# Feed-forward output product by seven block products in place of eight, in two of its three parts

## The chip, the cores and the metric

The kernel runs on one core of a Trainium2 chip. The metric is the device time of one launch in microseconds. Before the change the median of three runs is 2927.22 us (2925.56 to 2929.83).

## What is computed

A decoder trunk of two layers is applied to 512 prompt rows and to 8 sequences of 8 sample rows, 576 token columns in all, with a model width of 1024. Everything is float32. The change touches only the two feed-forward blocks of each layer:

```
D_MODEL = 1024
FFN_HIDDEN = 2816
def swiglu(x, w_in, w_out):
    gate, up = jnp.split(x @ w_in, 2, axis=-1)
    return (jax.nn.silu(gate) * up) @ w_out
...
x = x + 0.5 * swiglu(rms_norm(x, p['ffn1_norm']), p['ffn1_w_in'], p['ffn1_w_out'])
...                                   # mixers
x = x + 0.5 * swiglu(rms_norm(x, p['ffn2_norm']), p['ffn2_w_in'], p['ffn2_w_out'])
```

## The kernel before

Activations lie transposed: 128 channels on the partitions, 576 token columns (`N`) in the free dimension, two halves of 288 (`HF`). A float32 product is made of three products of rounded parts. Each weight tile and each activation is split into a high part (`whi`, `hh`, `ah`, a rounded copy by ScalarE) and a low part (`wlo`, `hl`, `al`, the original minus the high part, by VectorE); TensorE adds high x high, high x low and low x high (`project`, line 464). A tile is 128 output channels: for each of its chunks of 128 input channels three products in two halves, six matmuls of 288 columns. The two halves go to the two banks of one of four PSUM buffers `ps`.

Weights come in units of 1 MB (1024 x 256 values), two tiles each, into the two slots of `wraw` (`load`, line 356, on SyncE's queue). A unit is asked for when both tiles of the unit in the same slot have been split. Two slots of `whi` and `wlo` hold two split tiles; while TensorE works on one tile the tile two further on is split as soon as its slot is free (`split_ahead`, line 795 on ScalarE and line 1053 on VectorE).

The hidden width 2816 is worked off in three parts of 8, 8 and 6 chunks (`make_plan`). A part has a gates stage and an output stage. In the gates stage each step makes four tiles, two of the gate and two of the up projection; VectorE scales them by the row norm (line 1087), ScalarE takes Silu (line 827), VectorE multiplies (line 1095) and splits the result into `ah` and `al` (lines 1097, 1099). The output stage multiplies the part's chunks with `w_out` into eight output tiles, 8 chunks x 6 = 48 matmuls each, and VectorE adds half of each to `x` (line 1069). GpSimd only adds squares for the norms (line 1473) and issues stores. All order is written out by hand: each engine runs its own program in the order of the code, and semaphores (`filled`, `freed`, `lo_ready`, ...) tie them. After the first part of the first block SyncE also issues 16 small loads (`past_forgets`, line 382).

There are 2 layers x 2 blocks x 2 parts of 8 chunks: eight output stages with 1024 intermediate rows.

## Time and profile before

| | us |
|---|---|
| median of three runs | 2927.22 |
| the profiled execution's own time | 2922.63 |
| its span | 2921.0 |
| TensorE busy | 2876.8 (98%) |
| VectorE busy | 1462.1 (50%) |
| ScalarE busy | 986.9 (34%) |
| GpSimd busy | 118.5 (4%) |

The span is the time between the first and the last recorded instruction of the profiled execution; its own time is 1.6 us longer. Busy time counts an instruction's recorded duration; matmuls overlap each other in the pipeline, so the distance between two of them is shorter than the recorded duration of one.

### The profile page before, as it was taken

What the parts mean: (1) busy time and instruction counts of PE and PEld (TensorE: products, weight loads), DVE (VectorE), ACT (ScalarE), POOL (GpSimd) and SP (SyncE); (2) the same over time, 40 slices, a digit from 0 to 9 for tenths busy, and PEclk for the clock granted to TensorE, in tenths of its full rate; (3) what the DMA queues carried; (4) which work ended last, traced back from release to release, by engine and by line L of the source; (5) the groups of instructions that cost most, each with busy time, mean ns of one, the idle gap of its engine ahead of it and who ended that gap; (6) DMA issues with size and microseconds to landing.
All of it is one profiled execution on the core that took longest, in us unless ns stands there. A gap on an engine that the chain in (4) does not pass through costs nothing.

```text
span 2921.0 us, 55041 instructions
## 1 busy us (share of the span) xinstructions
PE 2876.8 (98%) x21664; PEld 2815.2 (96%) x21664; DVE 1462.1 (50%) x2025; ACT 986.9 (34%) x1295; POOL 118.5 (4%) x104
## 2 busy tenths in 40 slices
PE   7999999999999999999999999999999999999999
PEld 6999999898899999999999999998889999999998
DVE  4434356677545444343554343576665444444444
ACT  4212123555533332111332211335554333321124
POOL 1000001000000010000100000100000001000001
PEclk9999999999999999999999999999999999999999
DMA  3222223333222222222222222233332222222222
GB/s 119 86 75 84 87 72 99 89 93 89 79 79 86 86 87 76 83 86 74 86 83 78 87 87 86 73 89 89 95 102 67 86 79 94 77 83 87 84 75 90
DMA packets 299022, 248.82 MB, mean 85 GB/s; under 512 B 20643, under 2 KB 296307, under 8 KB 298919
## 3 DMA queue, kind: packets, MB, share of 16 engines
q1 hardware_dynamic: 296775, 242.44, 26.9%
q0 software_dynamic: 2144, 4.98, 0.5%
q8 instruction: 68, 1.11, 0.2%
q14 instruction: 35, 0.29, 0.0%
HBM read 240.04 MB, written 7.34 MB: 85 GB/s over the span
## 4 chain that ended last, share of the span: by engine, by line
PE 95%; DVE 2%; issue 1%; ACT 1%; DVEq 1%; DMA 0%; POOLq 0%; ACTq 0%; SPq 0%
PE ps L464 87%; PE ps L630 1%; PE ps L568 1%; PE ps L569 1%; PE ps L570 1%; PE ps L648 1%; PE ps L610 1%; DVE tmp L1059 1%; PE ps L695 0%; PE ps L617 0%; PE ps L632 0%; DMA xin<-in_x_sample 0%; PE ps L663 0%; ACT whi L795 0%; POOLq L1471 0%
## 5 line engine op out<-in xcount | busy, mean ns | idle before, releaser
L795 ACT ACTIVATE whi<-wraw 128x1024 fp32r<-128x1024 f32 x452 | 471.9, 1045 | 1554.6 <-PE ps L464 1542.7
L464 PE MATMUL ps<-hh,whi 128*128 128x288 f32 x4480 | 965.9, 297 | 11.7 <-DVE wlo L1053 5.3
L464 PE MATMUL ps<-hl,whi 128*128 128x288 f32 x4480 | 959.1, 296 | 0.0
L464 PE MATMUL ps<-hh,wlo 128*128 128x288 f32 x4480 | 959.1, 296 | 0.0
L1053 DVE TENSOR_TENSOR wlo<-wraw,whi 128x1024 fp32r<-128x1024 f32 x452 | 543.9, 1204 | 401.1 <-ACT whi L795 400.3
L464 PEld LDWEIGHTS ps<-hh,whi 128*128 128x128 f32 x4480 | 722.5, 189 | 14.5 <-DVE wlo L1053 6.3
L464 PEld LDWEIGHTS ps<-hl,whi 128*128 128x128 f32 x4480 | 722.7, 189 | 0.0
L464 PEld LDWEIGHTS ps<-hh,wlo 128*128 128x128 f32 x4480 | 722.3, 189 | 0.0
L1087 DVE TENSOR_TENSOR tmp<-tmp,ps 128x576 f32<-128x576 f32 x176 | 132.6, 753 | 505.3 <-PE ps L464 504.3
L464 PE MATMUL ps<-ah,wlo 128*128 128x288 f32 x1408 | 302.2, 296 | 0.0
L464 PE MATMUL ps<-ah,whi 128*128 128x288 f32 x1408 | 302.2, 296 | 0.0
L464 PE MATMUL ps<-al,whi 128*128 128x288 f32 x1408 | 302.1, 296 | 0.0
L1069 DVE SCALAR_TENSOR_TENSOR x<-ps,x 128x576 f32 x112 | 84.8, 757 | 351.7 <-PE ps L464 351.7
L464 PEld LDWEIGHTS ps<-ah,whi 128*128 128x128 f32 x1408 | 227.4, 189 | 0.0
L464 PEld LDWEIGHTS ps<-al,whi 128*128 128x128 f32 x1408 | 227.4, 188 | 0.0
L464 PEld LDWEIGHTS ps<-ah,wlo 128*128 128x128 f32 x1408 | 227.4, 188 | 0.0
L795 ACT ACT_TABLE_LOAD x32 | 41.1, 1283 | 143.6 <-PE ps L464 143.5
L1469 POOL COPY tmp<-tmp 128x576 f32<-128x576 f32 x7 | 6.7, 952 | 2039.9 <-ACT tmp L815 2024.6
L1473 POOL TENSOR_TENSOR tmp<-tmp 128x576 f32<-128x576 f32 x49 | 82.5, 1685 | 156.9 <-ACT tmp L815 155.3
L464 PE MATMUL ps<-ol,whi 128*128 128x288 f32 x384 | 82.5, 296 | 0.0
L464 PE MATMUL ps<-oh,whi 128*128 128x288 f32 x384 | 82.4, 296 | 0.0
L464 PE MATMUL ps<-oh,wlo 128*128 128x288 f32 x384 | 82.3, 296 | 0.0
(296 smaller groups left out, 2425.1 us busy)
## 6 DMA issues: line engine op xcount, KB each, us to landing
wraw<-in_ffn_w_in SPq DMA_DIRECT2D x88, 1024.0 KB
wraw<-in_ffn_w_out SPq DMA_DIRECT2D x32, 1024.0 KB
wraw<-in_w_in SPq DMA_DIRECT2D x28, 1024.0 KB
wraw<-in_w_in SPq DMA_DIRECT2D x56, 512.0 KB
wraw<-in_ffn_w_out SPq DMA_DIRECT2D x16, 768.0 KB
wraw<-in_w_branch SPq DMA_DIRECT2D x24, 512.0 KB
wraw<-in_w_out SPq DMA_DIRECT2D x9, 1024.0 KB
kv<-in_cache_k SPq DMA_DIRECT2D x128, 64.0 KB, 1.9
```

Of the source, the lines that this page charges most:

```text
L464: last = pe.matmul(ps[slot][:, half, 0:HF], weights, rhs[:, k, half * HF:(half + 1) * HF], start=(start and c == 0 and n == 0), stop=(stop ...
L568: pe.matmul(out, hh[:, k, tok], rh, start=(k == 0), stop=False)
L569: pe.matmul(out, hl[:, k, tok], rh, start=False, stop=False)
L570: last = pe.matmul(out, hh[:, k, tok], rl, start=False, stop=(k == KD - 1))
L610: last = pe.matmul(ps[pr.slot(k)][:, half, 0:HF], bones, tmp[k - 3][:, half * HF:half * HF + HF], start=True, stop=True)
L630: pe.matmul(logits(e, qb), qp[hs, qs], kp[hs, 0:n], start=True, stop=False, skip_group_check=True)
L648: last = pe.matmul(ps[pr.slot(k)][:, half, 0:XB // 2], wab[:, k - 13, :], tmp[3][:, half * (XB // 2):(half + 1) * (XB // 2)], start=True, ...
L795: act.activation(split_tile(into, j, rowwise), raw_tile(slot, j, rowwise), ACT.Copy).then_inc(hi_ready, 1)
L1053: dve.tensor_tensor(split_tile(lo, j, rowwise), raw_tile(slot, j, rowwise), split_tile(hi, j, rowwise).bitcast(F32), ALU.subtract).then_in ...
L1069: dve.scalar_tensor_tensor(out=two(xm), in0=cols(st.slot(k)), scalar=half, in1=two(xm), op0=ALU.mult, op1=ALU.add)\
L1087: dve.tensor_tensor(two(pf[:, 0:N]), two(tmp[6][:, 0:N]), cols(st_in.slot(k)), ALU.mult)\
L1473: pool.tensor_tensor(tmp[6][:, 0:N], tmp[6][:, 0:N], tmp[2 + m % 2][:, 0:N], ALU.add).then_inc(sq_added, 1)
```

## The change

In the first two parts of each block the output product (1024 outputs x 1024 intermediate rows x 576 columns) is done by Strassen's scheme. One unit of `w_out` (256 outputs x 1024 intermediate rows) is taken as 2 x 2 blocks of 128 outputs x 512 rows, the intermediate values as 2 x 2 blocks of 512 rows x 288 columns. Seven products of sums of blocks replace eight products of blocks. One product is 4 chunks x 3 parts = 12 matmuls of 288 columns, a unit is 84 matmuls in place of 96, a stage of four units 336 in place of 384.

- GpSimd makes the four sums of weight blocks (`weight_sums`) in `wsum`, one instruction of 512 elements each. A sum may overwrite its buffer when the low part of the former unit's has been made.
- ScalarE and VectorE split seven weight blocks of 512 elements per unit (`comb_split`) in place of two tiles of 1024, into a ring of four, four products ahead.
- The activations are kept as seven splits (`bh`, `bl`: B11, T1, T2, T3, B21, B22, T4, where T1 to T4 are differences) in place of `ah`, `al`. VectorE makes the differences and the low parts, ScalarE the high parts, in the gates stage (`gates_seven`). Chunks 0 to 3 hold the upper row blocks, so B11 and T1 are complete after them; the other five need chunks 4 to 7.
- The products run into three banks, `a`, `c` and `b`, in the order a, c, a, c, a, b, a. The partial sum in bank `a` or `c` is copied out by ScalarE (0.5 times it) before the next product adds to the same bank; VectorE adds banks and copies to `x` (`out_seven`). In total VectorE has, per unit, three additions of 288 elements from PSUM and three of copies (288, 576, 288), where it had two of 576.
- The next load of `w_out` is released when the last block of the unit two before has been split. The next stage's tiles are split after products 25 and 27.
- `lfp` moves to another place in SBUF, and VectorE waits for the state stores before the second block and not behind it.

```diff
+M_B11, M_T1, M_T2, M_T3, M_B21, M_B22, M_T4 = range(7)
+MOVING = (M_B11, M_T1, M_T2, M_B22, M_T3, M_B21, M_T4)
+DONE_NO = {0: 1, 1: 2, 2: 3, 4: 4, 5: 5}
+COPY_NO = {2: 1, 3: 2, 4: 3, 6: 4}
...
+            bh = sb("bh", [P, 7, 4, HF], F32R, m)
+            bl = sb("bl", [P, 7, 4, HF], F32R, m)
+            kept = sb("kept", [P, 4, 3, HF], F32, m)
+            wsum = sb("wsum", [P, 4, 4 * P], F32, m)
...
+        def ring(buf, q):
+
+            r = q % 4
+            return buf[:, r // 2, r % 2 * 4 * P:(r % 2 + 1) * 4 * P].rearrange("p (k c) -> p k c", c=P)
...
+            def seven(st, g, L):
+
+                for u in range(4):
+                    i, k0 = u // 2, 2 * (u % 2)
+                    first, second = ps[st.slot(k0)], ps[st.slot(k0 + 1)]
+                    a, b, c = first[:, 0, 0:HF], first[:, 1, 0:HF], second[:, 0, 0:HF]
+                    for m, bank in enumerate((a, c, a, c, a, b, a)):
+                        q = 7 * u + m
+                        if m < 6:
+                            pe.wait_ge(comb_lo, L * 96 + (24 * g + 6 * u + m + 1))
+                        else:
+                            pe.wait_ge(lo_ready, st.unit(0, L) * 2 + (2 * u + 2 + AHEAD))
+                        if m < 2:
+                            wait_psum(st, k0 + m, L, i)
+                        if m in COPY_NO:
+                            pe.wait_ge(part_copied, L * 64 + (16 * g + 4 * u + COPY_NO[m]))
+                        if q == 0:
+                            pe.wait_ge(mov_ready, L * 64 + (16 * g + 4))
+                        wh, wl = ring(whi, q), ring(wlo, q)
+                        x_ = MOVING[m]
+                        for kk in range(4):
+                            if u == 0 and m >= 2:
+                                pe.wait_ge(mov_ready, L * 64 + (16 * g + 4 + 3 * kk + (1 if x_ in (M_T2, M_T3) else 3 if x_ == M_T4 else 2)))
+                            for t, (weights, moving) in enumerate(((wh, bh), (wh, bl), (wl, bh))):
+                                last = pe.matmul(bank, weights[:, kk, :], moving[:, x_, kk, :], start=(m in (0, 1, 5) and kk == 0 and t == 0),
+                                                 stop=(m in (3, 5, 6) and kk == 3 and t == 2), skip_group_check=True)
+                        if m == 3:
+                            last.then_inc(filled[st.slot(k0 + 1)], 1)
+                        elif m == 6:
+                            last.then_inc(filled[st.slot(k0)], 1)
+                        else:
+                            last.then_inc(product_done, 1)
...
+            def comb_split(st, g, q, L):
+
+                u, m = divmod(q, 7)
+                if m in (0, 5, 6):
+                    raw_loaded(st, u, L)
+                else:
+                    act.wait_ge(wsum_ready, L * 64 + (16 * g + 4 * u + m))
+                ins = act.activation(ring(whi, q), weights_of(st, u, m), ACT.Copy)
+                if m < 6:
+                    ins.then_inc(comb_hi, 1)
+                else:
+                    ins.then_inc(hi_ready, 2)
...
+                for u in range(4):
+                    i, k0 = u // 2, 2 * (u % 2)
+                    first, second = ps[st.slot(k0)], ps[st.slot(k0 + 1)]
+                    one, other = scratch(u)
+                    for m in range(7):
+                        q = 7 * u + m
+                        if m == 3:
+                            wait_tile(st, k0 + 1, L, i)
+                        elif m == 6:
+                            wait_tile(st, k0, L, i)
+                        else:
+                            act.wait_ge(product_done, L * 80 + (20 * g + 5 * u + DONE_NO[m]))
+                        if m == 0:
+                            act.activation(one[:, 0:HF], first[:, 0, 0:HF], ACT.Copy, scale=0.5).then_inc(part_copied, 1)
+                        elif m == 1:
+                            act.activation(other[:, HF:N], second[:, 0, 0:HF], ACT.Copy, scale=0.5).then_inc(part_copied, 1)
+                        elif m == 2:
+                            act.activation(one[:, HF:N], first[:, 0, 0:HF], ACT.Copy, scale=0.5).then_inc(part_copied, 1)
+                        elif m == 4:
+                            act.activation(other[:, 0:HF], first[:, 0, 0:HF], ACT.Copy, scale=0.5).then_inc(part_copied, 1)
+                        if q == 1:
+                            moving_late(g, 3, L)
+                        if q + 4 < 28:
+                            comb_split(st, g, q + 4, L)
+                        elif q == 25:
+                            split_ahead(st, 2, None, L, 1)
+                        elif q == 27:
+                            split_ahead(st, 3, None, L, 1)
+                        if q == 0:
+                            moving_sums(g, 3, L)
...
+            def moving_lo(g, at, a, b, c, raw, L):
+
+                dve.wait_ge(mov_hi, L * 64 + (16 * g + at + 1))
+                dve.tensor_tensor(bl[:, a:b, c, :], raw, bh[:, a:b, c, :].bitcast(F32), ALU.subtract).then_inc(mov_ready, 1)
...
+            def gates_seven(st, st_out, g, s0, L):
+
+                for i in range(4):
+                    for k in range(4):
+                        wait_tile(st, k, L, i)
+                        pf = tmp[k if k < 2 else 2 + k]
+                        dve.tensor_tensor(two(pf[:, 0:N]), two(tmp[6][:, 0:N]), cols(st.slot(k)), ALU.mult).then_inc(freed[st.slot(k)], 1)
+                        if k < 2:
+                            split_ahead(st, k, L, i)
+                            continue
+                        c = 2 * i + k - 2
+                        dve.drain()
+                        dve.wait_ge(silu_ready, L * 44 + (s0 + i * 2 + k - 1))
+                        if c < 4:
+                            dve.tensor_tensor(kept[:, c, 0:2, :], two(pf[:, 0:N]), two(tmp[k - 2][:, 0:N]), ALU.mult)
+                            dve.drain()
+                            dve.tensor_tensor(kept[:, c, 2, :], kept[:, c, 1, :], kept[:, c, 0, :], ALU.subtract).then_inc(mov_raw, 1)
+                            split_ahead(st, k, L, i)
+                            moving_lo(g, c, M_B11, M_T1 + 1, c, kept[:, c, 0:3:2, :], L)
+                            continue
+                        kk = c - 4
+                        dve.tensor_tensor(pf[:, 0:N], pf[:, 0:N], tmp[k - 2][:, 0:N], ALU.mult)
+                        dve.drain()
+                        dve.tensor_tensor(tmp[2][:, 0:HF], pf[:, HF:N], kept[:, kk, 2, :], ALU.subtract)
+                        dve.tensor_tensor(tmp[2][:, HF:N], pf[:, HF:N], kept[:, kk, 1, :], ALU.subtract).then_inc(mov_raw, 1)
+                        dve.drain()
+                        dve.tensor_tensor(tmp[3][:, 0:HF], pf[:, 0:HF], tmp[2][:, 0:HF], ALU.subtract).then_inc(mov_raw, 1)
+                        if i < 3:
+                            split_ahead(st, k, L, i)
+                        else:
+                            comb_split(st_out, g, 2 * k - 4, L)
+                        moving_lo(g, 4 + 3 * kk, M_T2, M_T3 + 1, kk, two(tmp[2][:, 0:N]), L)
+                        if i == 3:
+                            comb_split(st_out, g, 2 * k - 3, L)
+                        moving_lo(g, 5 + 3 * kk, M_B21, M_B22 + 1, kk, two(pf[:, 0:N]), L)
+                        moving_lo(g, 6 + 3 * kk, M_T4, M_T4 + 1, kk, tmp[3][:, 0:HF].rearrange("p (a n) -> p a n", a=1), L)
...
+                        if m == 3:
+                            wait_tile(st, k0 + 1, L, i)
+                            dve.scalar_tensor_tensor(out=up[:, HF:N], in0=second[:, 0, 0:HF], scalar=0.5, in1=up[:, HF:N], op0=ALU.mult, op1=ALU.add)\
+                                .then_inc(freed[st.slot(k0 + 1)], 1)
+                        elif m == 5:
+                            dve.wait_ge(product_done, L * 80 + (20 * g + 5 * u + 5))
+                            dve.scalar_tensor_tensor(out=up[:, 0:HF], in0=first[:, 1, 0:HF], scalar=0.5, in1=up[:, 0:HF], op0=ALU.mult, op1=ALU.add)
+                            dve.wait_ge(part_copied, L * 64 + (16 * g + 4 * u + 4))
+                            dve.tensor_tensor(down[:, HF:N], down[:, HF:N], other[:, 0:HF], ALU.add)
+                            dve.drain()
+                            dve.tensor_tensor(up, up, one[:, 0:N], ALU.add)
+                            dve.tensor_tensor(down[:, HF:N], down[:, HF:N], other[:, HF:N], ALU.add)
+                        elif m == 6:
+                            dve.drain()
+                            wait_tile(st, k0, L, i)
+                            dve.scalar_tensor_tensor(out=down[:, 0:HF], in0=first[:, 0, 0:HF], scalar=0.5, in1=down[:, 0:HF], op0=ALU.mult, op1=ALU.add)\
+                                .then_inc(freed[st.slot(k0)], 1)
+                        if q + 4 < 28:
+                            comb_split(st, g, q + 4, L)
+                        elif q == 25:
+                            split_ahead(st, 2, L, 1)
+                        elif q == 27:
+                            split_ahead(st, 3, L, 1)
...
+                dve.wait_ge(f_stored, L * 96 + 96)
                 ffn("ffn2", 2, L)
-
-                dve.wait_ge(f_stored, L * 96 + 96)
 
...
+            def weight_sums(st, g, L):
+
+                for u in range(4):
+                    base = st.first_unit + u
+                    slot = base % 2
+                    a11, a12, a21, a22 = (block_of(slot, kh, mh_) for mh_ in range(2) for kh in range(2))
+                    wait_apart(pool, unit_loaded[slot], L * (plan["layer_units"] // 2 * 32) + (base // 2 + 1) * 32)
+                    for j, (x0, x1, op) in enumerate(((a21, a22, ALU.add), (summed(0), a11, ALU.subtract), (a12, summed(1), ALU.subtract),
+                                                      (a11, a21, ALU.subtract))):
+                        if u:
+                            wait_apart(pool, comb_lo, L * 96 + (24 * g + 6 * u - 4 + j))
+                        pool.tensor_tensor(summed(j), x0, x1, op).then_inc(wsum_ready, 1)
+                        pool.drain()
+
             add_squares(0)
             with pool.Fori(0, DEPTH) as L:
+                for part in range(2):
+                    weight_sums(S["ffn1"][part][1], part_no(0, part), L)
```

The order of the instructions at three places. First TensorE at the start of an output stage of 1024 rows, before (`ah` and `al` are the intermediate values, ps1 a PSUM buffer of two banks):

```order
L450 ISA [waits lo_ready]
L504 ISA [waits freed1]
L464 MATMUL ps1<-ah,whi 128x288 [waits a_ready]
L464 MATMUL ps1<-ah,whi 128x288
L464 MATMUL ps1<-al,whi 128x288 x2
L464 MATMUL ps1<-ah,wlo 128x288 x2
```

and now, where product 0 goes to ps1, product 1 to ps2 and product 2 to ps1 again:

```order
L494 REGISTER_ALU [waits comb_lo]
L543 REGISTER_ALU [waits freed1]
L550 MATMUL ps1<-bh,whi 128x288 [waits mov_ready]
...
L550 MATMUL ps2<-bh,whi 128x288 [waits freed2,comb_lo]
...
L541 REGISTER_ALU [waits comb_lo]
L548 REGISTER_ALU [waits part_copied]
L550 MATMUL ps1<-bh,whi 128x288 [waits mov_ready]
```

A product has 12 matmuls where a tile had 48, and each product waits for its own weight block (`comb_lo`) and from product 2 on for the copy of its bank (`part_copied`).

Second, VectorE from the last tile of a gates stage on, before (tmp5 is the up projection, tmp1 the Silu of the gate):

```order
L1087 TENSOR_TENSOR tmp5<-tmp6,ps0 128x576 [waits filled0]
L1094 REGISTER_ALU
L1095 TENSOR_TENSOR tmp5<-tmp5,tmp1 128x576 [waits silu_ready]
L1097 ISA
L1097 COPY ah<-tmp5 128x576
L1099 REGISTER_ALU
L1099 TENSOR_TENSOR al<-tmp5,ah 128x576
L1052 REGISTER_ALU
L1053 TENSOR_TENSOR wlo<-wraw,whi 128x1024 [waits hi_ready]
```

and now (the `wlo` rows are the low parts of the weight blocks of products 2, 3 and 4):

```order
L1268 TENSOR_TENSOR tmp5<-tmp6,ps0 128x576 [waits filled0]
...
L1283 TENSOR_TENSOR tmp5<-tmp5,tmp1 128x576 [waits silu_ready]
L1285 TENSOR_TENSOR tmp2<-tmp5,kept 128x288
L1286 TENSOR_TENSOR tmp2<-tmp5,kept 128x288
L1288 TENSOR_TENSOR tmp3<-tmp5,tmp2 128x288
...
L1251 TENSOR_TENSOR wlo<-wsum,whi 128x512 [waits comb_hi]
...
L1260 TENSOR_TENSOR bl<-tmp2,bh 128x2x288 [waits mov_hi]
...
L1251 TENSOR_TENSOR wlo<-wsum,whi 128x512 [waits comb_hi]
...
L1260 TENSOR_TENSOR bl<-tmp5,bh 128x2x288 [waits mov_hi]
...
L1260 TENSOR_TENSOR bl<-tmp3,bh 128x288 [waits mov_hi]
...
L1251 TENSOR_TENSOR wlo<-wsum,whi 128x512 [waits comb_hi]
```

Three differences and the low parts of three groups of activations stand between the tile and the weight blocks of products 2 to 4.

Third, GpSimd, which before had nothing in these stages; now the four sums of a stage's first unit and two of its second (`wsum` is written, `wraw` are the loaded weights):

```order
L1740 TENSOR_TENSOR wsum<-wraw 128x512 [waits unit_loaded0,pre_done]
L1740 TENSOR_TENSOR wsum<-wsum,wraw 128x512
L1740 TENSOR_TENSOR wsum<-wraw,wsum 128x512
L1740 TENSOR_TENSOR wsum<-wraw 128x512
L286 ISA [waits unit_loaded1,pre_done]
L1740 TENSOR_TENSOR wsum<-wraw 128x512 [waits comb_lo,pre_done]
L286 REGISTER_ALU
L1740 TENSOR_TENSOR wsum<-wsum,wraw 128x512 [waits comb_lo,pre_done]
```

The first unit's sums wait for its load alone; those of each later unit also for the low parts of the unit before.

## Rows read from the trace of the kernel before

**Rows 1.** The page: span, busy time by engine, granted clock in 40 slices.

```profile
span 2921.0 us, 55041 instructions
...
PE 2876.8 (98%) x21664; PEld 2815.2 (96%) x21664; DVE 1462.1 (50%) x2025; ACT 986.9 (34%) x1295; POOL 118.5 (4%) x104
...
PEclk9999999999999999999999999999999999999999
```

**Rows 2.** The page: chain that ended last, by engine and by line.

```profile
PE 95%; DVE 2%; issue 1%; ACT 1%; DVEq 1%; DMA 0%; POOLq 0%; ACTq 0%; SPq 0%
PE ps L464 87%; PE ps L630 1%; PE ps L568 1%; PE ps L569 1%; PE ps L570 1%; PE ps L648 1%; PE ps L610 1%; DVE tmp L1059 1%; PE ps L695 0%; PE ps L617 0%; PE ps L632 0%; DMA xin<-in_x_sample 0%; PE ps L663 0%; ACT whi L795 0%; POOLq L1471 0%
```

**Rows 3.** Timeline, TensorE, first output product and next gates (start us, us, what).

```profile
135.48 0.42 PE L464 MATMUL ps<-ah,whi 128*128 128x288 f32 x2
...
186.68 0.43 PE L464 MATMUL ps<-hh,whi 128*128 128x288 f32 x2
```

**Rows 4.** Timeline, VectorE, last gate tile and first output tile of that stage.

```profile
135.68 0.75 DVE L1087 TENSOR_TENSOR tmp<-tmp,ps 128x576 f32<-128x576 f32 x1 [1.80 <-PE ps L464]
136.60 0.76 DVE L1095 TENSOR_TENSOR tmp<-tmp 128x576 f32<-128x576 f32 x1 [0.16 <-issue]
...
138.15 0.76 DVE L1099 TENSOR_TENSOR al<-tmp,ah 128x576 f32 x1
138.83 1.22 DVE L1053 TENSOR_TENSOR wlo<-wraw,whi 128x1024 fp32r<-128x1024 f32 x1
142.20 0.76 DVE L1069 SCALAR_TENSOR_TENSOR x<-ps,x 128x576 f32 x1 [2.16 <-PE ps L464]
```

**Rows 5.** Timeline, ScalarE, a whole split and a Silu in the gates.

```profile
123.20 1.06 ACT L795 ACTIVATE whi<-wraw 128x1024 fp32r<-128x1024 f32 x1 [1.75 <-PE ps L464]
124.17 0.67 ACT L827 ACTIVATE tmp<-tmp 128x576 f32<-128x576 f32 x1
```

**Rows 6.** Timelines, VectorE and ScalarE near 540; last row by line: smaller shapes.

```profile
540.56 0.45 DVE L1356 TENSOR_TENSOR tmp<-tmp,ps 128x288 f32<-128x288 f32 x1
...
542.10 0.68 DVE L1053 TENSOR_TENSOR wlo<-wraw,whi 128x512 fp32r<-128x512 f32 x1
...
540.25 0.63 ACT L795 ACTIVATE whi<-wraw 128x512 fp32r<-128x512 f32 x1 [1.18 <-PE ps L464]
...
L892 ACT ACTIVATE vtok<-ps,small 128x256 f32<-128x256 f32 x20 | 7.9, 477 | 17.9 <-PE ps L570 17.7
```

**Rows 7.** Timelines, GpSimd and VectorE, end of the first row of squares.

```profile
26.50 1.40 POOL L1473 TENSOR_TENSOR tmp<-tmp 128x576 f32<-128x576 f32 x1 [0.16 <-issue]
...
27.65 1.34 DVE L1148 TENSOR_TENSOR wlo<-wraw,whi 128x1024 fp32r<-128x1024 f32 x1 [11.77 <-ACT whi L857]
```

**Rows 8.** Timelines, VectorE and GpSimd near 458; last row by tile: vlo (min/median/max ns).

```profile
457.94 0.82 DVE L1074 SCALAR_TENSOR_TENSOR hl<-x,gains,hh  x1
459.23 3.04 DVE L1053 TENSOR_TENSOR vlo<-wraw,vhi 128x1024 fp32r<-128x1024 f32 x2 [0.47 <-ACT vhi L795]
...
458.32 1.72 POOL L1473 TENSOR_TENSOR tmp<-tmp 128x576 f32<-128x576 f32 x1 [3.06 <-ACT tmp L815]
...
L1053 DVE TENSOR_TENSOR vlo<-wraw,vhi x4: 1212/1558/1904, 459.2 to 1901.0; 128x1024 fp32r<-128x1024 f32 x4
```

**Rows 9.** Timelines, SyncE queue; then windows of 1 us, last two columns DMA share, GB/s.

```profile
152.85 18.34 SPq L382 DMA_DIRECT2D lfp<-in_cache_logf  x16
...
189.45 0.40 SPq L356 DMA_DIRECT2D wraw<-in_ffn_w_in  x1
...
193.00:194.00 1.00, 1.00 (x10) 1.00 (x9) 0.74 (x1) 0.59 (x1) 0.00 (x0) 1.00 0.89 299
194.00:195.00 1.00, 1.00 (x10) 1.00 (x9) 0.51 (x2) 1.00 (x2) 0.00 (x0) 1.00 0.06 16
```

**Rows 10.** Timeline, TensorE, product of the values, 256 columns into one bank.

```profile
463.07 0.28 PE L570 MATMUL ps<-wlo,hh 128*128 128x256 f32 x1
463.19 0.28 PE L568 MATMUL ps<-whi,hh 128*128 128x256 f32 x1
463.31 0.28 PE L569 MATMUL ps<-whi,hl 128*128 128x256 f32 x1
```

More of the change, by code:

```diff
@@ L212, in build @@
                 cs = sb("cs", [P, PAST + ST], F32, m2)
-                lfp = sb("lfp", [P, NPG, 2 * NS], F32, m2)
                 lf = sb("lf", [F_W, N], F32, m2)
@@ L221, in build @@
                 prow = sb("prow", [P, NR], F32, m2)
+                lfp = sb("lfp", [P, NPG, 2 * NS], F32, m2)
             with ExitStack() as m2:
@@ L309, in split_tile, with block_of, summed, weights_of @@
             return buf[:, j, 0:n * P].rearrange("p (k c) -> p k c", c=P)
+        def ring(buf, q):
+            r = q % 4
+            return buf[:, r // 2, r % 2 * 4 * P:(r % 2 + 1) * 4 * P].rearrange("p (k c) -> p k c", c=P)
+        def block_of(u, kh, mh_):
+            return wraw[:, u, :].rearrange("p (k c) -> p k c", c=256)[:, 4 * kh:4 * kh + 4, mh_ * P:mh_ * P + P]
+        def summed(j):
+            return wsum[:, j, :].rearrange("p (k c) -> p k c", c=P)
+        def weights_of(st, u, m):
+            slot = (st.first_unit + u) % 2
+            if m == 0:
+                return block_of(slot, 0, 0)
+            if m == 5:
+                return block_of(slot, 1, 0)
+            if m == 6:
+                return block_of(slot, 1, 1)
+            return summed(m - 1)
+        def scratch(u):
+            return tmp[(0, 4)[u % 2]], tmp[(1, 5)[u % 2]]
+        def part_no(n, part):
+            return 2 * (n // 2) + part
         def ahead(st, k):
@@ L820, in ffn @@
                 for part, (st_in, st_out, kc) in enumerate(S[name]):
+                    if part < 2:
+                        gates_seven(st_in, st_out, part_no(n, part), L)
+                        out_seven(st_out, part_no(n, part), L)
+                        done += kc
+                        continue
                     with act.Fori(0, st_in.steps) as i:
@@ L1076, in update, with comb_split @@
                                 .then_inc(h_ready, 1)
+            def comb_split(st, g, q, L):
+                u, m = divmod(q, 7)
+                if m < 6:
+                    dve.wait_ge(comb_hi, L * 96 + (24 * g + 6 * u + m + 1))
+                else:
+                    dve.wait_ge(hi_ready, st.unit(0, L) * 2 + (2 * u + 2))
+                ins = dve.tensor_tensor(ring(wlo, q), weights_of(st, u, m), ring(whi, q).bitcast(F32), ALU.subtract)
+                if m < 6:
+                    ins.then_inc(comb_lo, 1)
+                else:
+                    ins.then_inc(lo_ready, 2)
@@ new lines, in out_seven @@
+            def out_seven(st, g, L):
+                for u in range(4):
+                    i, k0 = u // 2, 2 * (u % 2)
+                    first, second = ps[st.slot(k0)], ps[st.slot(k0 + 1)]
+                    one, other = scratch(u)
+                    up, down = x[:, 2 * u, :], x[:, 2 * u + 1, :]
+                    for m in range(7):
+                        q = 7 * u + m
+                        if m == 3:
[21 more added lines that the diff above has]
+                            split_ahead(st, 3, L, 1)
@@ L1081, in ffn @@
                 for part, (st_in, st_out, kc) in enumerate(S[name]):
+                    if part < 2:
+                        gates_seven(st_in, st_out, part_no(n, part), 22 * (n // 2) + done, L)
+                        out_seven(st_out, part_no(n, part), L)
+                        done += kc
+                        continue
                     with dve.Fori(0, st_in.steps) as i:
@@ L1515, in _ @@
                 add_squares(L * 24 + 16)
+                for part in range(2):
+                    weight_sums(S["ffn2"][part][1], part_no(2, part), L)
                 add_squares(L * 24 + 24)
```

61 lines of the change are left out of this document (49 added, 12 removed).

## The prediction

> **What bounds the kernel now.** I read the page first: TensorE is busy for 98% of the span at the full granted clock, VectorE for 50%, GpSimd for 4% [rows 1]. The chain that ended last is TensorE for 95%, nearly all at the one line of the split products [rows 2]. So a matmul fewer is time gained as long as TensorE's stream stays closed, and the other engines have spare time on average. The timeline of TensorE gives the price: the first output stage runs from 135.48 to 186.68, 51.20 us for 8 tiles x 48 = 384 matmuls, 133.3 ns each [rows 3], and VectorE, ScalarE and the loads wait for it. Then I read the timelines of VectorE and ScalarE at the stage's start for what stands between the last gate tile and the first products [rows 4, 5], the smaller shapes [rows 6], and the places where GpSimd and VectorE work at once [rows 7, 8], since the change makes them do so in every stage.
>
> **What goes.** Each of the eight stages loses 384 - 336 = 48 matmuls: 48 x 133.3 ns = 6.40 us, 51.2 us in all. The shape (288 columns, 128 x 128 weights, a weight load for each) is the same. One product is 12 matmuls, 1.60 us; a unit 11.2 us; a stage 44.8 us.
>
> The Trainium skill (TensorE: Matmul & The Clock Gate, Back-to-back issue gap) gives N/2.4 + 2.5 ns for a lone warm gap, 122.5 ns at 288 columns; by it the saving would be 47.0 us. The row has 133.3 ns, and I go by the row.
>
> **What each engine must do in a unit.** An instruction that follows another on VectorE starts about 0.08 us before the former's recorded end (138.15 + 0.76 against 138.83) [rows 4], so its cost in a row is 0.60 for 512 elements (0.68), 0.37 for 288 (0.45) and 0.68 for 576 (0.76) [rows 4, 6]. A wait for the pipe between dependent ones adds about 0.17 (136.60 after 135.68 + 0.75). VectorE: seven weight blocks 4.2, three additions from PSUM 1.1, three additions of copies 1.4, two such waits 0.3: 7.0 of 11.2 us. ScalarE: seven blocks of 0.55, four copies that I put at 0.4 (128x256 from PSUM took 0.48, 128x512 from SBUF 0.63 [rows 6]): 5.5 us. A copy has one product's time, 1.6 us, before its bank is needed: hidden. The longest row on VectorE, behind product 5, is 2.7 us and stands against the 4.8 us of three products by which the ring is ahead: hidden. GpSimd: a sum of 576 elements took 1.40 us beside an idle VectorE [rows 7]. I take 0.12 of it as start (below), 1.28 as work, and by elements 1.14 for 512. Not seen is whether a block read from `wraw` (128 of each 256 values) costs more; bounds are 1.14 (in proportion) and 1.60 (the 1.72 recorded for 576 in rows 8, less the start). I take 1.14, since the 1.72 is explained by a wait.
>
> **Loads.** A load was asked for at 189.45 and its last full window of traffic is 193 to 194 [rows 9]: about 4.6 us. The load of unit u+2 is now released at the end of product 7u+2 plus about 1.5 us and lands 6.1 us behind that product; ScalarE wants it after product 7u+10, 12.8 us behind. Covered. SyncE's 16 small loads hold its queue for 18.34 us once per layer [rows 9]; they now start near 153.5 and end near 172, the next stage's first unit lands near 177, and it is wanted at 135.5 + 26 x 1.6 = 177.1. Between nothing and 1 us, twice; I take 0. The stage's end: ScalarE can split the next gates' first tile from product 25's end on, VectorE is done 0.4 + 1.06 + 1.22 and some 0.15 for two hand-overs later [rows 4 to 6], 2.8 us against 3.2 until TensorE wants it: covered by 0.4. The earlier wait for the state stores and the place of `lfp` cost nothing: both are long over when asked for.
>
> **The stage's start, if engines didn't hinder each other.** Zero is the first product's start (135.48). VectorE takes up the last gate tile at 0.20 and begins the second multiplication at 1.12 [rows 4]. Then 0.76 and a wait of 0.19; two differences 0.37 + 0.45 + 0.17; the third 0.37; the low part of product 2's weights starts at 3.44 and ends at 4.12. TensorE wants it at 3.20 and goes on at 4.2: 1.0 us idle. Behind it in VectorE's row stand low parts of 576, 512, 576, 288, 512 elements; product 3's block is ready at 5.4 (wanted at 5.8), product 4's at 7.05 (wanted at 7.4). Net gain 6.4 - 1.0 = 5.4 us a stage.
>
> **What GpSimd's sums do to it.** The rows show each engine standing still while the other holds something. VectorE's 1024-element low part, median 1.22 us elsewhere, took 1.34 when begun at 27.65, and ended 1.09 behind GpSimd's end at 27.90 [rows 7]; of two begun at 459.23 (3.04 us in place of 2.36) the first waited for GpSimd, which ended at 460.04, and the tile's maximum is 1.90 against a minimum of 1.21 [rows 8]. The other way round, GpSimd's sum begun at 458.32 ended 1.28 us behind VectorE's end at 458.76 [rows 8]; alone it takes 1.40, hence the 0.12 above. All these have two inputs in SBUF; VectorE's PSUM readers are not among them.
>
> Per unit VectorE then needs the shared way for 4.2 + 1.4 = 5.6 us and GpSimd for 4 x 1.14 = 4.6: 10.2 of 11.2 us. That fits, and three products of lead soak up the turns once a stage runs. At its start there is no lead. The second unit's sums are released one by one by low parts 1, 2 and 3 of the first, so each comes at the worst time. Sum 0 takes the way from -0.45 to 0.69, the last low part of the gate chunk before goes behind it, and VectorE reaches the gate tile at 1.06 in place of 0.20: product 2's block is ready at 5.0, 1.8 us late. Sum 1 comes before product 3's block (ready at 7.4, wanted at 6.6 by now): 0.8. Sum 2 comes before the low part of T4 (product 4's block ready at 10.2, wanted at 9.0): 1.2. In all 3.8 us idle, a net gain of 6.4 - 3.8 = 2.6 us a stage.
>
> Rows 7 and 8 show one waiting instruction at a time; here VectorE has the next one ready when it ends, and the sum above lets the engine that has waited longer go first. The Trainium skill (SBUF — State Buffer, Who interferes with whom) says that whichever issues first has the shared pair for the whole instruction and the other blocks fully; by that the turns are as I took them, and the change comes to -21 us rather than the -43 of a VectorE that is never held up.
>
> **The sum.** 8 x (6.40 - 3.8) = 20.8 us. The profiled execution's 2922.6 becomes 2901.8; the median of the runs before lies 4.6 above that execution, so I say 2906.
>
> **Rivals.**
> First, VectorE isn't held up: its instructions follow so closely that GpSimd only gets in where VectorE waits anyway. For it: VectorE's instructions in a row overlap by 0.08 us. Against it: rows 7 and 8. It gives 8 x 5.4 = 43 us, 2884; if the 1.0 us goes too, 2876.
> Second, slower than before: GpSimd's sums are long and the shared way becomes the bound. At 1.60 us a sum the unit needs 5.6 + 6.4 = 12.0 us of it; the three units with sums of their own in the stage lose 0.8 each, and the start's three blockades grow by 0.46 each: 3.8 + 2.4 + 1.4 = 7.6 us against the 6.4 gained, +1.2 x 8 = 10 us, 2937. It decides from about 1.45 us a sum, where nothing is left. For it: the strided reads. Against it: 1.28 for 576 elements twice over.
> Third, gain and loss nearly cancel: sums of 1.3 to 1.4, or restarts of TensorE, late loads after the small ones and the narrow 0.4 us at each stage's end together take 1.5 to 2.6 us more a stage. It gives 2919 to 2927.
> Fourth, the products cost more than 133.3 ns a matmul, since 12 follow each other into one bank where before two banks took turns. Against it: in the values' product the matmuls of 256 columns all go to one bank and start 0.11 to 0.12 us apart [rows 10], 118.5 in proportion. I leave it a small chance inside the third case.
>
> **How the numbers follow.** Forecast 0.50 (2898 to 2915 on its own), first rival 0.20, third with fourth 0.18, second 0.12. A measurement tells 0.2%, 5.9 us, from no change. Faster: 0.50 + 0.20 + 0.06 = 0.76; same: 0.11 of the third case and 0.02 of the second, 0.13; slower: 0.11. The range from 2880 to 2932 takes in the first rival at 2884 and the third case, and leaves out the second rival's far end.
>
> **What would show it.** Output stages of 48 to 49 us (44.8 of products, the rest idle before products 2, 3 and 4 of the first unit, put down to VectorE's line 1251) show the sum right. VectorE's instructions there above 1.2 us with GpSimd beside them, and GpSimd's sums of 1.26 alone and up to 1.9 queued, show the shared way. Stages near 46 us speak for the first rival; idle time before products in units 2 and 3 with `wsum` behind it for the second; waits of ScalarE on a load for an error in the loads; a distance of matmuls over 134 ns within a product for the fourth. The prediction is wrong if the stall is not at the stage's start.

## The result, and the profile after

| | before | after |
|---|---|---|
| median of four runs, us | 2927.74 (2925.56 to 2929.83) | 2907.86 (2903.64 to 2909.55) |
| ratio, with its 95% interval | | 0.9933 (0.9919 to 0.9948) |
| profiled execution's span | 2921.0 | 2907.9 |

The forecast was 2906 us. The page of the kernel after answers to [rows 1, 2]:

```profile
span 2907.9 us, 56195 instructions
...
PE 2837.9 (98%) x21280; PEld 2770.5 (95%) x21280; DVE 1708.7 (59%) x2441; ACT 1131.7 (39%) x1683; POOL 312.1 (11%) x232
...
PE 88%; DVE 5%; issue 3%; SPq 1%; DVEq 1%; ACT 1%; DMA 1%; POOLq 0%; ACTq 0%
```

TensorE's share of the chain that ended last has gone from 95% to 88%, VectorE's from 2% to 5%. Of the 51.2 us of removed matmuls 18.5 are left in the eight stages of this execution (below); the rest, almost two thirds, has come back as waiting. Where it waits is seen in the timeline of TensorE through an undisturbed output stage (start us, us, what, and in brackets the idle time before with what ended it), which answers to [rows 3]:

```profile
290.65 0.29 PE L550 MATMUL ps<-bh,whi 128*128 128x288 f32 x1
...
295.49 0.39 PE L550 MATMUL ps<-bh,whi 128*128 128x288 f32 x1 [1.46 <-DVE wlo L1251]
...
297.83 0.39 PE L550 MATMUL ps<-bh,whi 128*128 128x288 f32 x1 [0.49 <-ACT tmp L966]
...
300.59 0.38 PE L550 MATMUL ps<-bh,whi 128*128 128x288 f32 x1 [0.91 <-DVE wlo L1251]
...
339.06 0.43 PE L508 MATMUL ps<-hh,whi 128*128 128x288 f32 x2
```

The stage takes 48.41 us, from 290.65 to 339.06, in place of 51.20. Counted from 0 as in the prediction, product 2 was due at 293.87 and began 1.62 late, product 3 (due 297.09) 0.74 late, product 4 (due 299.43) 1.16 late: 3.5 us idle. From there 24 products run without a gap in 38.47 us. Product 4 takes 1.67 of it, since a first matmul behind a stop takes some 0.08 longer; the other 23 take 1.600 each, 133.3 ns a matmul as before. VectorE and GpSimd over the same time, which answer to [rows 4, 8]:

```profile
288.78 0.68 DVE L1251 TENSOR_TENSOR wlo<-wsum,whi 128x512 fp32r<-128x512 f32 x1
289.38 2.21 DVE L1260 TENSOR_TENSOR bl<-tmp,bh 128x576 fp32r<-128x576 f32 x2
291.51 0.74 DVE L1268 TENSOR_TENSOR tmp<-tmp,ps 128x576 f32<-128x576 f32 x1
...
294.55 0.68 DVE L1251 TENSOR_TENSOR wlo<-wsum,whi 128x512 fp32r<-128x512 f32 x1
295.15 0.75 DVE L1260 TENSOR_TENSOR bl<-tmp,bh 128x576 fp32r<-128x576 f32 x1
295.82 1.79 DVE L1251 TENSOR_TENSOR wlo<-wsum,whi 128x512 fp32r<-128x512 f32 x1
297.53 2.22 DVE L1260 TENSOR_TENSOR bl<-tmp,bh 128x576 fp32r<-128x576 f32 x2
299.67 0.68 DVE L1251 TENSOR_TENSOR wlo<-wsum,whi 128x512 fp32r<-128x512 f32 x1
```

```profile
289.60 1.67 POOL L1740 TENSOR_TENSOR wsum<-wraw 128x512 f32<-128x512 f32 x1 [9.23 <-DVE wlo L1251]
295.38 1.67 POOL L1740 TENSOR_TENSOR wsum<-wsum,wraw 128x512 f32<-128x512 f32 x1 [4.11 <-DVE wlo L1251]
297.75 1.67 POOL L1740 TENSOR_TENSOR wsum<-wraw,wsum 128x512 f32<-128x512 f32 x1 [0.70 <-DVE wlo L1251]
```

The low part at 288.78 releases GpSimd's sum, which starts at 289.60 while VectorE is inside its next instruction. It waits for that one and then holds VectorE's following one until 291.27, so VectorE reads the last gate tile at 291.51. The same is seen at 295.82: a low part of 512 elements takes 1.79 in place of 0.68. It ends 0.56 behind the sum's end at 297.05. The third stop comes from the pair at 297.53, which takes 2.22 beside the sum at 297.75 (1.12 where no sum is read, below) and pushes back the low part at 299.67.

The bracket of product 3 names ScalarE's copy, but TensorE's program (`seven`) asks there only for the copy before that one. The three low parts end at 295.23, 297.61 and 300.35 and the products start 0.26, 0.22 and 0.24 later: all three waited for VectorE.

The eight output stages take, in order, 50.12, 48.41, 48.53, 48.40, 50.27, 48.39, 48.53, 48.43 us: 391.1 in place of 409.6. The first and the fifth, the ones of each layer with the 16 small loads, are 1.8 longer. SyncE's queue (two rows), ScalarE (one) and TensorE (one) at the end of the first, against [rows 9]:

```profile
161.69 18.38 SPq L426 DMA_DIRECT2D lfp<-in_cache_logf  x16
180.60 1.99 SPq L400 DMA_DIRECT2D wraw<-in_ffn_w_in  x2
```

```profile
185.70 2.04 ACT L875 ACTIVATE whi<-wraw 128x1024 fp32r<-128x1024 f32 x2 [1.85 <-DMA wraw<-in_ffn_w_in]
```

```profile
188.16 0.53 PE L508 MATMUL ps<-hh,whi 128*128 128x288 f32 x2 [1.56 <-DVE wlo L1219]
```

The small loads hold the queue until 180.07, the next gates' unit lands near 185.7, and TensorE stands still for 1.6 to 1.7 us.

**Where the profiled pair's 13.1 us come from.** The stages give 18.5. Two things work against it, by the distance of the gate tiles on VectorE (left out here: the rows between) in the first gates stage, before and after:

```profile
60.80 0.76 DVE L1087 TENSOR_TENSOR tmp<-tmp,ps 128x576 f32<-128x576 f32 x1 [1.81 <-PE ps L464]
...
67.04 0.75 DVE L1087 TENSOR_TENSOR tmp<-tmp,ps 128x576 f32<-128x576 f32 x1 [1.88 <-PE ps L464]
```

```profile
61.44 0.76 DVE L1268 TENSOR_TENSOR tmp<-tmp,ps 128x576 f32<-128x576 f32 x1 [2.37 <-PE ps L508]
...
67.84 0.76 DVE L1268 TENSOR_TENSOR tmp<-tmp,ps 128x576 f32<-128x576 f32 x1 [2.38 <-PE ps L508]
```

6.24 us a tile before, 6.40 after, at a granted clock of 1.00 in both: 2.56 us in each layer's first gates stage. At the start of layer 2 TensorE idled 1.9 us and then ran at 0.50 (1.2 GHz) for about 3.3 us, which cost 1.5 (24 matmuls of 288 columns took 4.81 us, and 3.29 behind the stop of 2.7 us at the same place in layer 1, where the clock stayed at 1.00):

```profile
1479.00:1480.00 1.00, 0.04 (x1) 1.00 0.00 0
1480.00:1481.00 1.00, 1.00 (x7) 0.85 0.00 0
1481.00:1482.00 1.00, 1.00 (x6) 0.50 0.00 0
...
1483.00:1484.00 1.00, 1.00 (x6) 0.50 0.63 181
1484.00:1485.00 1.00, 1.00 (x9) 0.94 1.08 383
```

(Columns: stretch, its length, TensorE busy, granted clock, DMA share, GB/s.) In layer 1 the stretch from the second output stage's end to the third's start, mostly mixers, is 1.4 shorter; in the second profile of the kernel before it is 1.1 shorter too, so most of that belongs to the execution. 18.5 - 5.1 - 1.5 + 1.4 = 13.3, near the 13.1. The medians differ by 19.9, near the 18.5 of the stages, and the second profiles of both kernels, at the end of the experiments, show why.

### The profile page after: what moved, and what is told of

It reads as the page before. It is cut to its first block, busy times and chain, and to the rows that moved or that the text cites. A ratio compares the mean times of both kernels' runs of the same rounds, so it can differ in the third digit from the quotient of the medians.

```text
span 2907.9 us, 56195 instructions
## 1 busy us (share of the span) xinstructions
PE 2837.9 (98%) x21280; PEld 2770.5 (95%) x21280; DVE 1708.7 (59%) x2441; ACT 1131.7 (39%) x1683; POOL 312.1 (11%) x232
## 3 DMA queue, kind: packets, MB, share of 16 engines
q8 instruction: 79, 1.29, 0.2%
## 4 chain that ended last, share of the span: by engine, by line
PE 88%; DVE 5%; issue 3%; SPq 1%; DVEq 1%; ACT 1%; DMA 1%; POOLq 0%; ACTq 0%
PE ps L508 72%; PE ps L550 8%; DVE bl L1260 1%; PE ps L710 1%; DVE wlo L1251 1%; PE ps L650 1%; PE ps L649 1%; PE ps L648 1%; PE ps L728 1%; PE ps L690 1%; SPq L426 1%; DVE tmp L1225 1%; SPq L424 1%; PE ps L775 0%; PE ps L697 0%
## 5 line engine op out<-in xcount | busy, mean ns | idle before, releaser
L875 ACT ACTIVATE whi<-wraw 128x1024 fp32r<-128x1024 f32 (+1 forms) x388 | 403.8, 1041 | 1144.4 <-PE ps L508 1118.0
L1219 DVE TENSOR_TENSOR wlo<-wraw,whi 128x1024 fp32r<-128x1024 f32 (+1 forms) x388 | 466.8, 1203 | 388.5 <-ACT whi L875 387.7
L550 PE MATMUL ps<-bh,whi 128*128 128x288 f32 x896 | 267.0, 298 | 23.0 <-DVE wlo L1251 18.9
L550 PE MATMUL ps<-bh,wlo 128*128 128x288 f32 x896 | 266.7, 298 | 0.0
L550 PE MATMUL ps<-bl,whi 128*128 128x288 f32 x896 | 265.2, 296 | 0.0
L550 PEld LDWEIGHTS ps<-bh,whi 128*128 128x128 f32 x896 | 168.4, 188 | 28.3 <-issue 28.3
L550 PEld LDWEIGHTS ps<-bl,whi 128*128 128x128 f32 x896 | 169.1, 189 | 0.0
L550 PEld LDWEIGHTS ps<-bh,wlo 128*128 128x128 f32 x896 | 168.3, 188 | 0.0
L1251 DVE TENSOR_TENSOR wlo<-wraw,whi 128x512 fp32r<-128x512 f32 x96 | 112.6, 1189 | 17.1 <-ACT whi L908 16.8
L1251 DVE TENSOR_TENSOR wlo<-wsum,whi 128x512 fp32r<-128x512 f32 x128 | 114.0, 893 | 6.7 <-ACT whi L908 6.1
```

Of the source, the lines that this page charges most:

```text
L550: last = pe.matmul(bank, weights[:, kk, :], moving[:, x_, kk, :], start=(m in (0, 1, 5) and kk == 0 and t == 0), stop=(m in (3, 5, 6) and ...
L875: act.activation(split_tile(into, j, rowwise), raw_tile(slot, j, rowwise), ACT.Copy).then_inc(hi_ready, 1)
L1219: dve.tensor_tensor(split_tile(lo, j, rowwise), raw_tile(slot, j, rowwise), split_tile(hi, j, rowwise).bitcast(F32), ALU.subtract).then_in ...
L1251: ins = dve.tensor_tensor(ring(wlo, q), weights_of(st, u, m), ring(whi, q).bitcast(F32), ALU.subtract)
```

## Experiments

All are timed beside the kernel before on the same chip. "Stages" is the sum of the eight output stages (before 409.6).

| | median us | ratio to before (95%) | stages us |
|---|---|---|---|
| after, again | 2906.72 | 0.9931 (0.9918 to 0.9944) | 391.4 |
| sums only written | 2885.77 | 0.9862 (0.9847 to 0.9877) | 370.6 |
| sums later | 2902.38 | 0.9912 (0.9897 to 0.9927) | 387.3 |
| small loads split | 2904.42 | 0.9925 (0.9911 to 0.9939) | 388.3 |
| sums twice | 2981.80 | 1.0190 (1.0175 to 1.0206) | 467.6 |
| sums on VectorE | 2886.95 | 0.9860 (0.9843 to 0.9876) | 372.1 |
| same, split, hoisted | 2887.91 | 0.9866 (0.9850 to 0.9883) | 372.1 |
| same, split | 2883.02 | 0.9851 (0.9838 to 0.9864) | 368.9 |

**Sums only written.** Is it GpSimd's reading that holds VectorE up, or only how late things are? GpSimd writes zeros twice in place of each sum, about as long; the weight sums are left out of the result.

```diff
-pool.tensor_tensor(summed(j), x0, x1, op).then_inc(wsum_ready, 1)
+pool.memset(summed(j), 0.0)
+pool.drain()
+pool.memset(summed(j), 0.0).then_inc(wsum_ready, 1)
```

> The changed kernel, but GpSimd writes zeros twice where it made each sum of weight blocks (the sums are left out), so its instructions there take about as long and read nothing from SBUF. Theory A (VectorE's two-input instructions stand still while GpSimd reads SBUF, and that is 2.4 us of the 3.4 us of idle time at each stage's start): no VectorE instruction of line 1251 or 1260 in the output stages takes over 0.8 us, idle time before products 3 and 4 is gone, 1.0 us is left before product 2, output stages of 46.0 us, and the time is 8 x 2.4 = 19 us under the changed kernel's 2908, about 2889. Rival B (the order in VectorE's queue alone makes the stall, and GpSimd only runs beside it): stages stay at 48.4 us, 2908.

Measured 2885.77; a stage without small loads takes 45.85 to 46.20 us, 1.0 us of idle time before product 2 left. The timelines there:

```profile
290.97 0.75 DVE L1260 TENSOR_TENSOR bl<-tmp,bh 128x576 fp32r<-128x576 f32 x1
291.17 0.53 POOL L1740 MEMSET wsum<- 128x512 f32 x1 [3.96 <-DVE wlo L1251]
291.27 0.40 PE L550 MATMUL ps<-bh,whi 128*128 128x288 f32 x1 [0.79 <-DVE wlo L1251]
...
292.24 1.12 DVE L1260 TENSOR_TENSOR bl<-tmp,bh 128x576 fp32r<-128x576 f32 x2
```

VectorE's instructions keep their 0.75, and 1.12 for two, with GpSimd's beside them; no low part of 512 elements in the output stages takes over 0.70, where in the kernel after 80 take over 0.8. The sums' reading costs 20.5 us of stages, 22 of the median. By the Trainium skill (SBUF — State Buffer, Who interferes with whom) a VectorE instruction with two inputs in SBUF contends with a GpSimd instruction that reads SBUF and not with one that only writes; this run agrees.

**Sums later.** The second unit's sums all wait for the low part of product 4's weights; they come one after another behind the stage's start.

```diff
-wait_apart(pool, comb_lo, L * 96 + (24 * g + 6 * u - 4 + j))
+wait_apart(pool, comb_lo, L * 96 + (24 * g + 6 * u - 4 + (3 if u == 1 else j)))
```

> The changed kernel with one wait moved: the second unit's four sums are released all by the low part of product 4's weights instead of one by one by those of products 1 to 4. Theory A: the shared way is free while VectorE works off the last gate tile; idle time before products 2, 3, 4 falls from 1.6 + 0.7 + 1.1 to 1.0 + 0 + 0 us, stages of 46.0 to 46.4 us, 16 to 19 us under the changed kernel, 2889 to 2892. If the sums are then too late for the second unit (wanted by ScalarE from product 4's end on, four sums at 1.7 us each): new idle time before products 8 to 11, up to 1.5 us a stage, 2900. Rival B: no change, 2908.

Measured 2902.38. The start's idle time is down to 1.0 us before product 2, but new idle times of 1.3 and 0.4 stand before products 9 and 10, since the three additions to `x` each wait for a sum (0.45, 0.76 and 0.45 when alone). VectorE, GpSimd, TensorE:

```profile
303.77 1.18 DVE L1316 TENSOR_TENSOR x<-x,tmp 128x288 f32<-128x288 f32 x1
305.02 1.73 DVE L1318 TENSOR_TENSOR x<-x,tmp 128x576 f32<-128x576 f32 x1
306.68 1.54 DVE L1319 TENSOR_TENSOR x<-x,tmp 128x288 f32<-128x288 f32 x1
```

```profile
304.85 1.29 POOL L1740 TENSOR_TENSOR wsum<-wraw 128x512 f32<-128x512 f32 x1 [0.22 <-issue]
```

```profile
308.87 0.40 PE L550 MATMUL ps<-bh,whi 128*128 128x288 f32 x1 [1.14 <-DVE wlo L1251]
```

A later start moves the turns; it does not remove them. Both halves of Theory A came true, and what is left of its 16 to 19 us is 5.5 (2907.86 to 2902.38; 3.8 of stages).

**Small loads split.** Eight of the 16 small loads are issued behind the first part, where all 16 stood, and eight behind the second part.

```diff
-if name == "ffn1" and done == 0:
-    past_forgets(L)
+if name == "ffn1" and done < 16:
+    past_forgets(L, range(4) if done == 0 else range(4, SB))
```

> The changed kernel, with the 16 small loads of the forget cache issued in two halves, 8 behind the loads of the first part and 8 behind those of the second. Theory A (the next gates' first load waits 18 us behind them in SyncE's queue, lands at 185.6 us and holds TensorE up for 1.7 us once per layer): the first output stage of each layer falls from 50.2 to 48.4 us, no idle time at its end, 3.5 us under the changed kernel, 2904. Rival (the load would be late without them too, since its release comes 12 us later than before): the stage stays at 50.2 us, or the second one grows by as much, 2908.

Measured 2904.42; the two long stages are 48.40 and 48.57 now, the gates' load is issued at 172.17 in place of 180.60. So the 1.7 and 1.9 us above were the queue's. Its 3.4 us on the median are less than the two intervals tell apart; the stages show it. (The profiled execution itself took 2895.09; three of its gates stages have the 6.24 us distance, worth 7.7 of the 9.3 that it lies under the median.)

**Sums twice.** Each sum is made twice, and nothing else is changed.

```diff
+pool.tensor_tensor(summed(j), x0, x1, op)
+pool.drain()
 pool.tensor_tensor(summed(j), x0, x1, op).then_inc(wsum_ready, 1)
```

> The changed kernel, with each of GpSimd's sums made twice, one behind the other (same values). Per unit GpSimd then needs the shared way for 8 x 1.14 = 9.1 us and VectorE for 5.6 us, 14.7 us against 11.2 us of products. Theory A (exclusive use is the limit once the sum of both passes the products): the three later units take about 14.7 us each, stages of 44.8 + 3 x 3.5 + 5 at the start = 60 us, 8 x 12 = 95 us over the changed kernel, about 3000. If GpSimd's own row of two sums a product (2 x 1.45 = 2.9 us, 11.6 us a unit) were the limit and the engines didn't hinder each other: stages of 47 to 49 us, 2900 to 2912.

Measured 2981.80, stages of 57.65 to 59.67. Where both engines always have an instruction ready, they take turns, one instruction each; only VectorE's additions from PSUM (line 1310) keep their 0.44 beside a running sum. GpSimd, VectorE, and TensorE before product 2 of the same stage:

```profile
319.33 1.29 POOL L1740 TENSOR_TENSOR wsum<-wraw 128x512 f32<-128x512 f32 x1 [4.33 <-DMA wraw<-in_ffn_w_out]
320.76 1.55 POOL L1742 TENSOR_TENSOR wsum<-wraw 128x512 f32<-128x512 f32 x1
```

```profile
319.83 3.03 DVE L1251 TENSOR_TENSOR wlo<-wsum,whi 128x512 fp32r<-128x512 f32 x2
322.79 3.49 DVE L1251 TENSOR_TENSOR wlo<-wraw,whi 128x512 fp32r<-128x512 f32 x2
326.20 0.44 DVE L1310 SCALAR_TENSOR_TENSOR x<-ps,x 128x288 f32<-128x288 f32 x1
```

```profile
304.54 0.40 PE L550 MATMUL ps<-bh,whi 128*128 128x288 f32 x1 [2.54 <-DVE wlo L1251]
```

Pairs of low parts that take 1.28 alone take 3.03 and 3.49. The loss was forecast too high (60 us a stage, 3000) and spread too evenly: the four units of this stage take 19.5, 11.3, 16.0 and 11.8 us, where 14.7 was expected for each of the last three. This is the state that the second rival feared, and one sum of 1.29 a block is short of it.

**Sums on VectorE.** GpSimd's four sums a unit go to VectorE, one between two low parts.

```diff
+def weight_sum(st, g, u, j, L):          # on VectorE
+    ...
+    dve.drain()
+    if j == 0:
+        dve.wait_ge(unit_loaded[slot], ...)
+    dve.tensor_tensor(summed(j), x0, x1, op).then_inc(wsum_ready, 1)
 ...
+if u < 3 and 1 <= m < 5:                 # in out_seven
+    weight_sum(st, g, u + 1, m - 1, L)
 ...
-    weight_sums(S["ffn1"][part][1], part_no(0, part), L)      # on GpSimd
```

> The changed kernel with the four sums of weight blocks on VectorE in place of GpSimd: those of the first unit behind the second tile of the last gates step, those of each later unit one behind each of the weight blocks split at products 1 to 4 of the unit before. VectorE's own work in a unit rises from 7.0 to 7.0 + 4 x (0.60 + 0.17) = 10.1 of 11.2 us. Theory A (what costs is two engines at one way, not VectorE's amount of work): 1.0 us idle before product 2, about 0.4 before product 9, where VectorE is behind with the first unit's work, stages of 46.2 us and 48 in each layer's first, 2.3 us x 8 = 18 us under the changed kernel's 2908, 2890. Rival B (VectorE with 10.1 of 11.2 us is the new bound, since its rows come in bursts): 1 us idle in every unit, stages of 49 to 50 us, 2912 to 2920.

Measured 2886.95. A sum takes VectorE 0.69, half of GpSimd's 1.29, and TensorE stops only before product 2 (1.0 us), in two stages before product 9 (0.25), and for the small loads at the end of each layer's first stage (2.0 to 2.1):

```profile
296.13 0.69 DVE L1251 TENSOR_TENSOR wlo<-wraw,whi 128x512 fp32r<-128x512 f32 x1
296.90 0.69 DVE L1266 TENSOR_TENSOR wsum<-wraw 128x512 f32<-128x512 f32 x1
```

```profile
PE 2835.9 (98%) x21280; PEld 2771.6 (96%) x21280; DVE 1702.8 (59%) x2569; ACT 1131.9 (39%) x1683; POOL 118.5 (4%) x104
```

VectorE's busy time is 1702.8 us with 128 instructions more than the 1708.7 of the kernel after: there some 90 us of it were waiting.

**The same with the small loads split** (the edit of that experiment on top of this one).

> The sums on VectorE and the 16 small loads in two halves, without the moved weight block. From the parts: all eight stages at 45.9 to 46.2 us, so 2 x 1.8 = 3.6 us under the version with the sums on VectorE alone (2887), 2883. Rival (the first stage of each layer has another delay beside the loads, as the 46.7 of the version with the moved block suggests): first stages at 46.6 us, 2885.

Measured 2883.02 (2880.46 to 2885.53, five runs), stages of 45.85 to 46.43. It beats both kernels: 1.5% under the one before, 0.8% under the one after.

**The same, and one low part earlier.** On top, VectorE makes product 2's low part right behind the scaling of the last gate tile, ahead of the differences.

```diff
+    if i == 3:
+        comb_split(st_out, g, 2 * k - 4, L)    # behind the scaling
 ...
-else:
-    comb_split(st_out, g, 2 * k - 4, L)        # behind the differences
```

> The sums on VectorE, the 16 small loads in two halves, and the low part of product 2's weights (and of product 0's) moved up to right behind the scaling of the gate tile. Theory A, from the parts: stages of 46.2 less 0.5 us (product 2's block is ready at 1.6 us, but T2 and T3 of the last chunk come 0.4 us later and are wanted at 4.4), all stages alike: 45.7 us, 8 x 2.7 + 3.4 = 25 us under the changed kernel, 2883. Rival B (VectorE's order at the start doesn't matter, T2's low part is as late as the weights): 46.2 us a stage, 2887.

Measured 2887.91, the rival's number, with stages of 46.2 to 46.8. TensorE is stopped inside product 2 now (0.6 us in most stages, and 0.3 before product 3), by the low parts of the moving side that the hoisted instruction has pushed back:

```profile
290.03 0.40 PE L550 MATMUL ps<-bh,whi 128*128 128x288 f32 x1 [0.46 <-DVE bl L1271]
```

Both operands of product 2 come from the same chain on VectorE; its order only chooses which is late. So the last 1.0 us a stage is put down to the length of that chain; no run shortened it.

**Before and after again,** for the distance of the gate tiles and the difference of the profiled pair.

> The kernel before, unchanged, for a second profile. In the first profile of it the gate tiles of each layer's first stage followed each other every 6.24 us, in the changed kernel's every 6.40 us. Theory C (that distance changes from one execution to the next, whatever the kernel): here some or all of them at 6.40, span 2921 to 2928. Rival D (the change made these tiles slower, 2 x 16 x 0.16 = 5.1 us given back): 6.24 again, and 6.40 in every version of the changed kernel.

> The changed kernel, unchanged, to tell its time on the same chip as the version with the sums on VectorE, and to see what of a profile repeats. The idle times of an output stage should repeat (stages of 48.4 and 50.2 us), since waits make them; the distance of the gate tiles of a layer's first stage (6.24 or 6.40) and a stretch at 1.2 GHz behind a stage's gap should not. Time 2904 to 2910.

```profile
61.33 0.76 DVE L1087 TENSOR_TENSOR tmp<-tmp,ps 128x576 f32<-128x576 f32 x1 [1.96 <-PE ps L464]
...
67.73 0.76 DVE L1087 TENSOR_TENSOR tmp<-tmp,ps 128x576 f32<-128x576 f32 x1 [2.03 <-PE ps L464]
```

The unchanged kernel before has 6.40 here too, a span of 2924.5 and a time of 2926.14. The execution with 6.24 was a lucky one by 3.5 us. The hoisted version shows both in one execution, 6.24 in layer 1 and 6.40 in layer 2, and it isn't bound to a layer's first stage: the version with sums only written has 6.24 in the first gates stage of both layers and of layer 1's second block, the one with the small loads split in three such stages (not in the very first), and the second profile of the kernel after in one gates stage (from 1628 us) where all other executions have 6.40. So the distance belongs to the execution and not to the change.

## Why the prediction was right, step by step

- **Removed matmuls, 6.40 us a stage.** Right: the remaining products take 1.600 us each. The fourth rival (a bank without turns costs more) is refuted: 133.3 ns a matmul, as before.
- **Stall at the stage's start, 3.8 us before products 2, 3 and 4.** Right in place, cause and size: 1.62 + 0.74 + 1.16 = 3.5 against 1.8 + 0.8 + 1.2. With the reads gone, or the sums on VectorE, 1.0 is left, the number worked out for engines that don't hinder each other.
- **VectorE held up by GpSimd, first come first served.** Right; it ruled the first rival out (2884 forecast for it, and 2885.77 measured where the hindrance was taken away).
- **A sum's length, 1.14 of work, 1.26 recorded.** 1.29 measured; the strided read of `wraw` costs nothing to speak of. It is short of the 1.45 where the second rival was said to take all (by the prediction's own terms, three later units at 4 sums each and three blockades, nothing is left from 1.52 on), and the doubled sums show that rival's mechanism as real, if weaker than its arithmetic: 1.9% slower.
- **The small loads, "nothing to 1 us, twice", taken as 0.** This was the term mis-sized: 1.7 and 1.9 us. The later start (138.04) and the stall of 3.5 move the loads and what wants them alike. But the margin was 0.1 us, and two terms were too short. The small loads began 23.65 us behind the stage's first product (161.69 less 138.04), where 18.0 and the stall make 21.5: the load before them was asked for at 159.84, 0.8 later than product 9's end plus 1.5, since the two low parts in front of it took 2.38 in place of 1.28, held up by a sum, and the first small load follows that load by 1.85 (before the change too), where about 0.5 was put; and the unit took 5.1 us from its issue at 180.60 to 185.70, where 4.6 was taken. That is 2.6 us in all, of which ScalarE, busy until 183.85, waited 1.85 and TensorE 1.7. Splitting the small loads gave the time back.
- **The stage's end, covered by 0.4 us.** Right: the other six stages end without a gap.
- **Sum.** 8 x 2.6 = 20.8 forecast. The runs have 6 x 2.75 and twice 1.0: 18.5. The 4.6 us added for the difference between the profiled execution and the median held, for a reason that was not known: that execution had 6.24 in the first gates stage of both layers, worth 5.1. That the forecast of 2906 lies within 2 us of the 2907.86 is in part luck: six stages gained 0.15 more than forecast, two 1.6 less, and the 4.6 was added without a known cause.
- **Third rival (2919 to 2927).** Refuted; its late loads are real, but 3.4 us in all.

## What to carry to other kernels

A two-input elementwise instruction on GpSimd is not free beside a busy VectorE: count its full length against VectorE's queue at the place where VectorE has no lead, and give it to VectorE outright if that has the room (0.69 us against 1.29, and some 20 us in this kernel). Where a stage gets shorter, look at the queues whose length stays: 16 small transfers of 1.15 us each had been hidden by a stage of 51 us and were not by one of 48. Compare times by medians, and a profiled pair stage by stage, before a difference of 0.2% in the rest of the program is put down to the change.

## What the runs showed of the hardware

- An instruction's recorded time holds its waiting for the other engine: VectorE's low part of 0.68 is recorded with up to 1.79 when a sum runs, and the busy share rises with it, so a page with a higher share of VectorE can be one with less work.
- Two engines with instructions always ready alternate one by one; neither starves, although VectorE's follow each other with an overlap of 0.08 us.
- GpSimd writing alone (128x512 in 0.53 us) leaves VectorE's times unchanged.
- The distance of gate tiles has two values, 6.24 and 6.40 us, at a granted clock recorded as 1.00 in both. It changes between executions and between gates stages of one, and three stages of it are worth 7.7 us. Its cause stays open.
- In some executions the granted clock fell to 0.50 (1.2 GHz) after a stop of TensorE at a layer's start, and stayed there for some 3 us; in others it didn't, and the length of the stop alone doesn't tell which. In the kernel after it fell behind 1.9 us of idle time in layer 2 and stayed at 1.00 behind 2.7 us in layer 1; in the kernel before it stayed at 1.00 behind 3.0 us. The fastest version fell behind 2.2 us in layer 1 (0.50 from 49 to 51 us) and not in layer 2, where its stop was under 1 us. Each fall cost about 1.5 us. Stops made by the kernel can bring it on too: the version with the sums on VectorE fell to 0.50 behind its waits for the small loads (from 187 and from 1610 us). Why one stop is followed by it and another isn't stays open.
